# Block products for four V tiles and for the last pair of down tiles of a hybrid decoder layer

## What is computed

```
xn = rmsnorm(x, g1)
q, k, v, o, ig, fg, u, vb, ga, gb = split_in(xn @ w_in)
h, C, n, m = mlstm_branch(q, k, v, ig, lf, C, n, m)      # chunks of 128, decay matrices, state per head
y_a = (sigmoid(o) * h) @ w_a
y_b = spatial_gate(gelu(u), rmsnorm(gelu(vb), g_v), w_s, b_s) @ w_b
x = x + (sigmoid(ga) * y_a + sigmoid(gb) * y_b) @ w_o
a, gval = split(causal_conv(rmsnorm(x, g2) @ w_up))
x = x + (silu(a) * gval) @ w_down
return rmsnorm(x, g_final)
```

## Time and profile before

| | |
|---|---|
| median of three runs | 895.54 us |
| profiled execution, its time | 896.04 us |
| profiled execution, its span | 894.2 us |
| PE busy | 886.6 us (99%) |
| DVE busy | 609.9 us (68%) |
| ACT busy | 390.5 us (44%) |
| POOL busy | 133.0 us (15%) |
| granted clock of PE, mean | 0.996 |
| memory traffic | 112 GB/s over the span |

### The profile page before, as it was taken

How to read it: one execution, slowest core, us unless ns; L and a number is a source line. 1 busy time by engine, 2 the same in 40 slices (tenths; PEclk the granted TensorE clock), 3 DMA queues, 4 the chain that set the end, 5 groups by cost and what they waited for, 6 DMA issues and landing times.

```text
span 894.2 us, 18963 instructions
## 1 busy us (share of the span) xinstructions
PE 886.6 (99%) x7306; PEld 881.9 (99%) x7306; DVE 609.9 (68%) x980; ACT 390.5 (44%) x629; POOL 133.0 (15%) x182
## 2 busy tenths in 40 slices
PE   9999999999999999999999999999999999999997
PEld 9999999999999999999999999999999999999997
DVE  7886775443885568677755777777777778966543
ACT  7545434544873334344432344444444444432333
POOL 0673000002542110000005800000000000000001
PEclk9999999999999999999999999999999999999998
DMA  6332252234872222322255222222222222333232
GB/s 214 107 131 89 77 196 101 84 100 149 291 269 69 67 76 75 116 95 95 96 197 135 89 81 94 94 94 94 94 93 86 83 91 87 99 107 93 85 106 96
DMA packets 31499, 100.44 MB, mean 112 GB/s; under 512 B 4668, under 2 KB 7260, under 8 KB 31192
## 3 DMA queue, kind: packets, MB, share of 16 engines
q1 hardware_dynamic: 29256, 92.96, 31.1%
q0 software_dynamic: 1472, 5.72, 2.1%
q10 hardware_dynamic: 720, 1.04, 0.4%
HBM read 92.37 MB, written 7.35 MB: 112 GB/s over the span
## 4 chain that ended last, share of the span: by engine, by line
PE 91%; POOLq 3%; issue 3%; DMA 1%; POOL 1%; ACT 0%; SPq 0%; ACTq 0%
PE out L1961 84%; PE trp L1961 3%; PE aux L1961 2%; POOLq L1939 2%; POOLq L1937 1%; PE trp L1995 1%; DMA cwb<-in_conv_wb 1%; DMA raw_pair<-in_w_slots 1%; PE aux L2153 0%; POOL y L1952 0%; POOL out_conv_old L1923 0%; ACT xg L581 0%; POOL sct L1927 0%; POOLq L1930 0%; POOLq L88 0%
## 5 line engine op out<-in xcount | busy, mean ns | idle before, releaser
L581 ACT ACTIVATE whi<-raw_pair 128x1024 fp32r<-128x1024 f32 (+4 forms) x168 | 154.2, 924 | 207.4 <-PE out L1961 195.6
L1083 DVE TENSOR_TENSOR wlo<-raw_pair,whi 128x1024 fp32r<-128x1024 f32 (+1 forms) x121 | 155.2, 1282 | 86.8 <-ACT whi L581 86.4
L1961 PE MATMUL out<-xh,whi 128*128 128x260 f32 x668 | 143.5, 289 | 0.0
L1961 PE MATMUL out<-x2h,whi 128*128 128x260 f32 x704 | 141.8, 283 | 0.0
L1961 PE MATMUL out<-x2l,whi 128*128 128x260 f32 x704 | 141.3, 282 | 0.0
L1961 PE MATMUL out<-x2h,wlo 128*128 128x260 f32 x704 | 141.2, 282 | 0.0
L1961 PE MATMUL out<-xl,whi 128*128 128x260 f32 x668 | 139.0, 282 | 0.0
L1961 PE MATMUL out<-xh,wlo 128*128 128x260 f32 x668 | 139.0, 282 | 0.0
L1961 PEld LDWEIGHTS out<-x2h,whi 128*128 128x128 f32 x704 | 108.4, 188 | 0.1
L1961 PEld LDWEIGHTS out<-x2h,wlo 128*128 128x128 f32 x704 | 108.3, 188 | 0.0
L1961 PEld LDWEIGHTS out<-x2l,whi 128*128 128x128 f32 x704 | 108.3, 188 | 0.0
(11 more groups left out here) (362 smaller groups left out, 1758.0 us busy)
## 6 DMA issues: line engine op xcount, KB each, us to landing
raw_pair<-in_w_slots SPq DMA_DIRECT2D x123, 512.0 KB, 3.3
raw_pair<-in_w_dn SPq DMA_DIRECT2D x16, 448.0 KB, 3.3
c_ring<-in_C_state SPq DMA_DIRECT2D x8, 512.0 KB, 5.1
row<-scratch SPq DMA_DIRECT2D x8, 512.0 KB, 5.9
out_C_sample<-c_ring SPq DMA_DIRECT2D x8, 512.0 KB, 4.3
raw_pair<-in_w_dn SPq DMA_DIRECT2D x8, 512.0 KB, 3.5
xres<-in_x_all POOLq DMA_DIRECT2D x1, 1560.0 KB, 6.8
x<-in_x_all SPq DMA_DIRECT2D x5, 260.0 KB, 6.7
```

Source lines behind the costliest of these rows:

```text
L581: return act.activation(out, in_, func, **kw_)
L1083: TT(wlo[p][:, 0:width], raw[p][:, 0:width], whi[p][:, 0:width].bitcast(F32), ALU.subtract)\
L1961: return pe.matmul(*a, **k)
```

## The change

1. V tiles 2 and 3, and V tiles 6 and 7, become two pairs of seven products (`VPair`). V tiles 0, 1, 4 and 5 stay whole. The loop over the V tiles is written out.
2. The combinations of x for these pairs are made by POOL during K: four sums of `xh` and `xl` and four differences, each 128 x 1040, into `vtf`. ACT copies them to `vth` (`v_combination_hi`), DVE subtracts to `vtl`, in place (`v_combination_low`). Three of the four DVE steps stand between the last `low` of K and `k_side(3)`, and because `vtl` lies on `vtf` they wait until POOL is through.
3. `vtf` lies where `c_ring` does. So the first four sample states and three broadcast rows are no longer loaded before or during V, but one by one as the last V pair finishes with each combination.
4. Products and sums of the sample normaliser n move from DVE to POOL.
5. Down tiles 6 and 7 become a fourth `DownPair` for contraction steps 0 to 7. `last_tile` keeps steps 8 to 21. The multiplication by the final gain (`dn_gained`) moves into the pairs, in place in `x1`. On DVE the second part's sum (`part_result(1)`) now comes before the first part's y (`part_y(0)`).

Of the diff, what the prediction speaks of:

```diff
             for h in range(NH):
                 if h >= 1:
                     k_side(h - 1)
                 low(At(S_K + h + 2))
+            v_combination_low(0, 1)
+            v_combination_low(1, 2)
+            v_combination_low(2, 3)
             k_side(NH - 1)
...
+            def v_combination_low(r, at):
+                dve.wait_ge(s_th, at)
+                dve.wait_ge(s_bt, min(at + 2, 4))
+                TT(vtl[:, V_AT[r], :, :], vtf[:, V_AT[r], :, :], vth[r][:, :, :].bitcast(F32), ALU.subtract).then_inc(s_tl, 1)
...
+            pool.wait_ge(s_xn, KT)
+            x_sum(2, 0, 1)
+            x_sum(1, 0, 0)
+            pool.drain()
+            x_difference(1, 2, 1)
+            x_sum(0, KT // 2, 1)
+            pool.drain()
+            x_difference(2, 0, 2)
+            pool.drain()
+            x_difference(0, 0, 1)
+            x_sum(3, KT // 2, 0)
+            pool.drain()
+            x_difference(3, 3, 0)
...
+            k_side(NH - 1)
+            v_combination_hi(3, 4)
+            v_plain(0)
...
-            tile(At(S_V + 1), xh, xl, mid=lambda: transposes(At(B_V), At(S_V)), end=sample_rows)
-            with pe.Fori(1, 4) as i:
-                for t in range(2):
-                    tile(At(S_V + t, i, 2), xh, xl,
-                         mid=lambda: transposes(At(B_V + t - 1, i, 2), At(S_V + t - 1, i, 2)))
-            tile(At(S_O), xh, xl, mid=lambda: transposes(At(B_V + 7), At(S_V + 7)))
+            tile(At(S_V + 1), xh, xl, mids={3: lambda: v_transposes(0), 5: sample_rows})
+            block_pair(pairs_v[0], lambda: v_transposes(1))
+            tile(At(S_V + 4), xh, xl, halves=1, mids={2: lambda: v_transposes(2), 3: lambda: v_transposes(3)})
+            tile(At(S_V + 5), xh, xl, mid=lambda: v_transposes(4))
+            block_pair(pairs_v[1], lambda: v_transposes(5))
+            tile(At(S_O), xh, xl, halves=2, mids={2: lambda: v_transposes(6), 3: lambda: v_transposes(7)})
...
+            pr = pairs_v[-1]
+            sp.wait_ge(s_pd, 6 * pr.v + 4)
+            load_row(0)
+            load_state(0)
+            sp.wait_ge(s_pl, 7 * pr.v + 7)
+            sp.dma_start(raw[pr.t1][:, :], wp[S_O + 1]).then_inc(w_loaded[pr.t1], 16)
...
-DOWN_PAIRS = 3
+DOWN_PAIRS = KT // 2
...
             part_scale(0)
+            part_result(1)
+            dve.wait_ge(s_xg, 1)
+            dve.wait_ge(s_rp, 1)
             part_y(0)
-            part_result(1)
```

More of the change, by code:

```diff
@@ L298, in __init__ @@
                 self.q = GATE_PAIRS + i
+                self.v = V_PAIRS + self.q
                 self.i, self.j = i, 2 * i
-                self.n = [At(S_DN + 6 * i + t) for t in range(8)]
+                self.last = i == DOWN_PAIRS - 1
+                self.n = [At(S_DN + 6 * i + t - (2 if self.last else 0)) for t in range(8)]
                 self.t0, self.t1 = self.n[4].c % 2, self.n[5].c % 2
@@ L314, in hybrid_layer @@
         pairs_w = [Pair(q) for q in range(GATE_PAIRS)]
+        pairs_v = [VPair(v) for v in range(V_PAIRS)]
         def vb_slot(j):
@@ L740, in k_side, with factor_hi, first_factors_hi, next_factors_hi @@
                 A(k_tok[:, :, h, :], trp[h % 2][:, :, :]).then_inc(tre[h % 2], 1)
+            def factor_hi(pr, f):
+                A(pr.place(whi, f), pr.factor[f]).then_inc(s_ch, 1)
+            def first_factors_hi(pr):
+                act.wait_ge(w_loaded[pr.t0], pr.n[0].half(1) * 16)
+                act.wait_ge(done, pr.n[0]())
+                factor_hi(pr, 0)
+                factor_hi(pr, 1)
+            def next_factors_hi(pr):
+                act.wait_ge(done, pr.n[1]())
+                act.wait_ge(s_sw, 4 * pr.v + 4)
+                factor_hi(pr, 2)
+                factor_hi(pr, 3)
+            def v_combination_hi(r, at):
+                act.wait_ge(s_bt, at)
+                A(vth[r][:, :, :], vtf[:, V_AT[r], :, :]).then_inc(s_th, 1)
             for h in range(NH):
@@ L775, in _ @@
-            for t in range(2):
[L776 to L786, removed]
+                if h == 2:
+                    v_combination_hi(0, 1)
@@ L845, in x_combination_hi @@
             def x_combination_hi(r):
-                act.wait_ge(s_bt, r + 1)
+                act.wait_ge(s_bt, 4 + r + 1)
                 A(th[:, r, :, :], tf[:, r, :, :]).then_inc(s_th, 1)
[L850 to L858, removed]
-                factor_hi(pr, 1)
-            def next_factors_hi(pr):
-                act.wait_ge(done, pr.n[1]())
-                act.wait_ge(s_sw, 4 * pr.q + 4)
-                factor_hi(pr, 2)
-                factor_hi(pr, 3)
             def by_plain(i):
@@ L1360, in _, with sample_exponents @@
-            low(At(S_V + 5))
-            with dve.Fori(2, 4) as i:
-                for t in range(2):
-                    low(At(S_V + t + 2, i, 2))
+            def sample_exponents():
+                dve.wait_ge(s_ss, 32)
+                TT(R(9), R(1), R(2), ALU.add)
+                dve.drain()
+                TT(R(3), R(9), R(0), ALU.max)
+                dve.drain()
+                TT(R(4), R(9), R(3), ALU.subtract)
+                TT(R(5), R(0), R(3), ALU.subtract)
+                TS(R(6), R(3), -1.0, None, ALU.mult).then_inc(s_sg, 1)
@@ L1746, in down_pair @@
                 result()
-                low(n[7], down_width(1 if pr is pairs_d[-1] else 2))
+                low(n[7], down_width(2))
                 ready(n[5])
-                dn_sum(j + 1)
+                if pr.last:
+                    TT(part(1, 0), part(1, 0), pr.p4, ALU.add)
+                else:
+                    dn_sum(j + 1)
                 dve.drain()
@@ L1755, in down_pair @@
                 TT(part(1, 1), part(1, 1), dtmp[:, 0, :], ALU.add)
-                result()
+                if not pr.last:
+                    result()
             dve.wait_ge(s_nc, 2 * FT)
@@ L1961, in MM, with tile @@
                 return pe.matmul(*a, **k)
-            def tile(n, hi, lo, k0=0, nk=KT, bank=None, use=None, start=True, stop=True, mid=None, mid_at=3, each=None, end=None, mids=None):
+            def tile(n, hi, lo, k0=0, nk=KT, bank=None, use=None, start=True, stop=True, mid=None, mid_at=3, each=None, end=None, mids=None, halves=None):
                 p = n.c % 2
-                pe.wait_ge(w_lo, n(1))
+                if halves is None:
+                    pe.wait_ge(w_lo, n(1))
+                else:
+                    pe.wait_ge(s_nl, halves)
                 if start:
@@ L1972, in tile @@
                         pe.wait_ge(each, k + 1)
+                    if halves is not None and k == KT // 2:
+                        pe.wait_ge(w_lo, n(1))
                     w = slice(k * P, (k + 1) * P)
@@ L2295, in down_pair @@
                 banks = [(S_DN + t) % 2 for t in range(2)]
-                for s in range(4):
+                slots = n[2:4] if pr.last else n[0:4]
+                for s, m in enumerate(slots):
                     t, g = s // 2, 1 + s % 2
```

520 lines of the change are left out of this document (307 added, 213 removed).

## The result

The changed kernel took **911.88 us** (median of 4 runs, 911.36 to 912.61), the kernel before 895.59 in the same session (4 runs, 895.25 to 895.70). Ratio 1.0181, 95% interval 1.0169 to 1.0194: slower by 16.3 us. The prediction was 896.7, with a range up to 899.6. A slower kernel was within its chances (0.42), the size far outside its range.

What follows compares the result with a forecast made beforehand. PE was taken as the bound, busy 886.6 of 894.2 us. Terms -2.8 + 3.4 + 0.2 + 0.5 - 0.1 = +1.2 us gave 896.7 us for the median, range 893.7 to 899.6 (the forecast's own 895.6 to 898.0).

Steps and rivals of the forecast that it cites:

- Term 1: V: two pairs need fewer matmuls than four whole tiles, -2.8 us if PE never waits.
- Term 2: K and V: POOL's combinations delay DVE, PE idles 3.4 us before V0's transposes; DVE slowed in K adds 0.2.
- rival 1: K: POOL is in time, at most 2.8 us per operation; stall 1.3 us, time 894.0 us; chance 0.24.
- Term 3: Start of O: sample states and rows move together with O1's and O2's weights, O2's land late, +0.5 us.
- Rival 3: O: the link is the bound, late states delay every unit, +3 us on top, 899.7 us; chance 0.08.
- Rival 2: V1: the clock falls behind PE's stall, if that is over about 2 us; 898.5 us; chance 0.25.
- Term 4: Last down tiles: part 0 ends later, part 1 earlier, but y's stores limit the end; -0.1 us.

Runs made afterwards that it cites:

- e1: Changed kernel with POOL's eight combination operations right behind its sums of squares (about 75 to 97 us) instead of during K: 915.15 us.
- e6: Changed kernel with POOL's second tq waiting until DVE has written wv: 909.87 us.
- e8: e7 with DVE computing wvq and wv ahead of the low part of O1's weights and clearing state behind it: 901.95 us.
- e9: e8 with O2's weights earlier in the queue, the sample exponents first behind K's last head, and POOL's second tq behind wv: 897.82 us.
- e7: Changed kernel with V's combinations made by DVE itself in U's pauses, and the three subtractions behind K's last head: 903.47 us.
- e10: e9 with the down tiles as before the change: 897.90 us.
- e5: Kernel before with only the down part of the change (fourth pair, weighting inside the pairs, last tile in two parts): 896.18 us against 895.65.
- e11: e9 with DVE's four subtractions around V1 spread instead of together, the first ahead of K's last head: 894.78 us against 895.91, ratio 0.9985.
- e12: e10 with DVE's order around V1 changed as in e11: 894.96 us against 895.91, ratio 0.9987.
- e4: e1 plus eight POOL additions at the old place in K, results unused, each cut into four instructions: 922.91 us (uncut 923.08).

## Why the prediction was wrong

**What bounds the kernel:** right. PE is the bound, and every microsecond lost was PE idle or at the low clock.

**Term 1, -2.8 us:** right; -2.71 between V0's and V7's transposes.

**Term 2, +3.4 at V1's middle:** the mechanism I described was harmless. POOL ended at 168.5, not 171.5, and e1, where nothing of POOL is late, has exactly the floor I gave, 1.3 us for the three subtractions ahead of the last `d_arg`. "I am wrong if POOL takes under 2.8 us each" came true, and yet it was not rival 1: the time went elsewhere.

**The step that failed** is the next one: "POOL also slows DVE's own work of K by perhaps 0.8 us for each disturbed operation, where PE has about 2 us of room per head ... +0.2 us". I took contention to slow POOL, since its means in the earlier trace rows were longer beside a busy DVE, and charged DVE a token. It is an exclusion, each way. One 0.35 us instruction waited 2.5 us, and a DVE queue with many short two-input instructions is held again and again. Waits at two of the four `d_arg` of a head added 4.3 us, and one `wlo` held over two additions 5.2, where the room was 2. Measured: +13.15 us up to V0's transposes in place of +3.6, of which 9.8 are the three waits of PE in the list above (8.5 and 1.3), about 0.6 a wait in 149 to 152 us, where PE was busy 2.43 of 3 us, and most of the rest the clock: eight `aux` matmuls took 2.07 us at 161.25 and 1.16 at 172.75 in the chain. Some 0.8 us I can't place. The trace of before had the sign of it: a `wlo` took 3.32 us in place of 1.23, beside POOL's `tq`:

```profile
205.48 3.32 DVE L1083 TENSOR_TENSOR wlo<-raw_pair,whi 128x1024 fp32r<-128x1024 f32 x1 [4.95 <-ACT whi L581]
```

```profile
205.28 2.44 POOL L1893 TENSOR_TENSOR tq<-c_ring,row 128x1024 f32<-128x1024 f32 x1 [1.15 <-DMA row<-scratch]
```

I had it in view and did not use it, because PE was not waiting there.

**Term 3, +0.5 in O:** +5.30. Its step was right and came late; another one decided. The sum priced O2's weights as the last transfer (9.5 us against 8.4) and had no term for `wv`, on which `kv`, `c_ring` and O2's `low` hang. By experiment: `wv` held by `tq` is worth 2.0 us of time and 3.0 of O in the trace (e6); the rest is its place behind O1's `low` (whose weights landed 6.06 us after their issue) and the memset, and behind that O2's weights (e8). With all three mended O is back at 44.21 us (e9), so all of the 5.30 is accounted for. Rival 3, every unit late by its state, did not come. Rows 9 were read a slice early: the link is at its rate from 228.5 us on, not from 225, where its slice shows 121 GB/s; no number of the sum hung on it.

**Rival 2, the clock:** it did fall, to 0.50 behind waits of 6.1 and 3.5 us. For shorter waits its condition ("over about 2 us") does not hold up. Waits of 2.1 and 0.7 us were followed by 0.89 in e7 and by 1.00 in e8 (185 to 200 us), a wait of 2.7 us by 1.00 in e9 and by 0.89 in e10, and K's second wait, 2.4 us, by 1.00. The length of the wait alone does not decide there.

**Term 4, -0.1:** +0.3 in the profile (the transposes ahead of the last pairs stand 15.51 us later than before, 858.61 to 843.10, and the span ends 15.8 later), +0.5 by e5 with an interval that holds a ratio of 1. Right within what can be told.

**Where the gain went, and what stays open:** of V's 2.8 us, 2.35 are seen in e11's trace (41.80 us from V0's to V7's transposes, 176.89 to 218.69, against 44.15). 0.90 are given back at the first two units of the branch stage, whose intervals grew from 3.75 and 3.96 to 4.16 and 4.45 us. There DVE comes late from its last updates of `c_ring`, and by the rows the lock has a part in that once more (not tested): beside `tq` at 256.58 eight of them (256.82 on) took 4.18 us, where before they took 2.80.

With 0.13 lost in O that leaves 1.3 us, less what the down part costs (0 to 0.5, e5), beside the 1.1 measured. It is one execution, and the slowest of e11's eleven (896.60 us), so this agreement is rough; e12's trace, which has 1.38 us more in O than before, does not show the gain that its median has. What decides between the two outcomes of the clock behind one and the same wait I did not settle. How K would behave with POOL's work in a place where DVE only reads PSUM was not tried; this kernel has none long enough.

## What to carry to other kernels

Before moving work to an idle GpSimd, list the VectorE instructions that will start while it runs: each one with two SBUF inputs (and, as e1's TENSOR_SCALAR shows, some with one) can wait for a whole GpSimd instruction, however small it is itself, so the price is up to the count of such starts times GpSimd's instruction length, set against the slack of whatever waits for VectorE. An instruction in the old trace that takes two or three times its usual duration beside the other engine is that price, shown for free, even where nobody waits for it. And when a first wait is removed, read the chain again: here `wv`, then O2's transfer, then four subtractions stood behind it.

## What was unexpected of the hardware

- The lock takes no account of size: VectorE operations on 4 partitions (0.34 to 0.69 us) took 2.5 to 2.8 us each beside 128 x 1040 additions, and GpSimd products on only 8 partitions lengthened 1.15 us subtractions to 1.7 on average.
- GpSimd copies (one SBUF input, 1040 elements) take 1.07 us alone and hold VectorE as well, up to 1.14 us at a time.
- The granted clock came back to 1.00 within 4 to 6 us of PE's return in K (161.25 to 166) and in O (242.6 to 248), and such a stall of PE cost some 2 us more than itself.
- Cutting GpSimd's additions into quarters (e4) shortened the longest single wait of a `d_arg` from 2.52 to 0.86 us and raised the median from 0.35 to 0.82; the time stayed (923.08 and 922.91 us).
